# Two units of the first projection moved ahead of the last block of modulation products

## The reference: what is computed

```
shift, scale, gate       = split(silu(c)     @ w_ada + b_ada, 3)      # w_ada: 2048 x 6144
shift_c, scale_c, gate_c = split(silu(c_ctx) @ w_ada + b_ada, 3)
hc = rmsnorm(ctx, g_pre) * (1 + scale_c) + shift_c
zc = hc @ w_in[:, :XBC_W + DT_W]
hx = rmsnorm(x, g_pre) * (1 + scale) + shift
zx = hx @ w_in
```

## Time and profile before

| | |
|---|---|
| three runs | 1981.38 us median (1978.72 to 1981.75) |
| profiled execution | 1981.05 us, its span 1979.2 us |
| PE busy | 1924.8 us, 97% of the span |
| DVE, ACT, POOL busy | 1210.3, 999.0, 102.9 us |
| DMA | 360.39 MB, mean 182 GB/s over the span |
| granted TensorE clock | 0.993 of full speed over the span |
| prefix (until phase B1 starts on PE) | 158.56 us of the span |

### The profile page before, as it was taken

How to read it: one execution, slowest core, us unless ns; L and a number is a source line. 1 busy time by engine, 2 the same in 40 slices (tenths; PEclk the granted TensorE clock), 3 DMA queues, 4 the chain that set the end, 5 groups by cost and what they waited for, 6 DMA issues and landing times.

```text
span 1979.2 us, 27905 instructions
## 1 busy us (share of the span) xinstructions
PE 1924.8 (97%) x10557; PEld 1637.6 (83%) x10557; DVE 1210.3 (61%) x1703; ACT 999.0 (50%) x1464; POOL 102.9 (5%) x117
## 2 busy tenths in 40 slices
PE   5889999989999999999999999999999999999999
PEld 3558888888888888887888998888889999998887
DVE  3335645676548888867866576767555454555554
ACT  5434322344555666754445433566544555556642
POOL 1010000000013344000000000000000000000000
PEclk8999999999999999999999999999999999999999
DMA  9973322347657666657975545545555655555554
GB/s 342 349 243 114 100 75 85 89 146 235 192 168 199 175 179 192 223 181 254 357 252 153 156 139 149 175 135 149 176 188 175 184 164 169 169 162 169 170 190 161
DMA packets 210040, 360.39 MB, mean 182 GB/s; under 512 B 14264, under 2 KB 61776, under 8 KB 209024
## 3 DMA queue, kind: packets, MB, share of 16 engines
q1 hardware_dynamic: 200448, 349.36, 56.7%
q10 hardware_dynamic: 8848, 8.47, 1.8%
q0 software_dynamic: 624, 0.92, 0.2%
HBM read 356.55 MB, written 2.16 MB: 181 GB/s over the span
## 4 chain that ended last, share of the span: by engine, by line
PE 87%; DMA 4%; DVE 3%; SPq 2%; ACT 1%; issue 1%; POOL 1%; ACTq 0%; POOLq 0%; DVEq 0%
PE acc L656 50%; PE acc L643 15%; PE acc L623 10%; DMA raw_first<-in_w_ada 2%; SPq L502 1%; DMA ex_a<-acs_scratch 1%; PE side L1026 1%; DVE w_lo L1912 1%; PE side L901 1%; DVE conv L2079 1%; PE side L718 1%; PE side L796 1%; PE side L893 1%; PE side L954 1%; PE side L623 1%
## 5 line engine op out<-in xcount | busy, mean ns | idle before, releaser
L1912 DVE TENSOR_TENSOR w_lo<-raw,w_hi 128x1024 fp32r<-128x1024 f32 (+1 forms) x552 | 674.5, 1227 | 428.3 <-ACT w_hi L1234 421.7
L1234 ACT CAST w_hi<-raw 128x1024 fp32r<-128x1024 f32 (+1 forms) x544 | 560.8, 1035 | 608.3 <-PE acc L656 414.7
L656 PE MATMUL acc<-w_hi,h_hi 128*128 128x512 f32 (+1 forms) x1312 | 522.6, 398 | 3.2 <-DVE h_lo L2278 1.8
L656 PE MATMUL acc<-w_hi,h_lo 128*128 128x512 f32 (+1 forms) x1312 | 509.1, 388 | 0.0
L656 PE MATMUL acc<-w_lo,h_hi 128*128 128x512 f32 (+1 forms) x1312 | 507.5, 387 | 0.0
L656 PEld LDWEIGHTS acc<-w_hi,h_lo 128*128 128x128 f32 x1312 | 246.3, 188 | 52.4
L656 PEld LDWEIGHTS acc<-w_hi,h_hi 128*128 128x128 f32 x1312 | 246.8, 188 | 50.4 <-DVE h_lo L2278 2.1
L656 PEld LDWEIGHTS acc<-w_lo,h_hi 128*128 128x128 f32 x1312 | 247.0, 188 | 47.0
L643 PE MATMUL acc<-h_hi,w_hi 128*128 128x256 f32 x896 | 258.3, 288 | 7.0 <-DVE w_lo L1912 5.5
L643 PE MATMUL acc<-h_lo,w_hi 128*128 128x256 f32 x896 | 254.4, 284 | 0.0
L643 PE MATMUL acc<-h_hi,w_lo 128*128 128x256 f32 x896 | 254.4, 284 | 0.0
(11 more groups left out here) (409 smaller groups left out, 2031.9 us busy)
## 6 DMA issues: line engine op xcount, KB each, us to landing
raw<-in_w_in SPq DMA_DIRECT2D x184, 512.0 KB, 4.3
raw<-in_w_in_odd SPq DMA_DIRECT2D x128, 512.0 KB, 3.7
raw<-in_w_in_even SPq DMA_DIRECT2D x96, 512.0 KB, 3.7
raw<-in_w_out SPq DMA_DIRECT2D x64, 512.0 KB, 5.0
raw_first<-in_w_ada SPq DMA_DIRECT2D x58, 512.0 KB, 8.8
gate_w<-in_w_ada SPq DMA_DIRECT2D x32, 512.0 KB, 6.7
raw<-in_w_out_even SPq DMA_DIRECT2D x32, 512.0 KB, 3.6
raw<-in_w_out_odd SPq DMA_DIRECT2D x32, 512.0 KB, 3.7
```

What stands on the lines that cost most here:

```text
L656: o = nc.tensor.matmul(ACC[b][:, 0:n], l, r, start=first and kk == 0 and m == 0, stop=last and kk == 1 and m == 2)
L1234: act.copy(WHI[:, u % 4, :, 0:n], RAW[:, u % 4, :, 0:n]).then_inc(hi_ready, 1)
L1912: dve.tensor_tensor(WLO[:, u % 4, :, 0:n], RAW[:, u % 4, :, 0:n], WHI[:, u % 4, :, 0:n].bitcast(F32), ALU.subtract).then_inc(lo_ready, 1)
```

## The change

PE multiplies units 11 and 12 ahead of the products of block 7, and the transposes of block 7 come right behind its products. DVE writes the low part of unit 12 ahead of its copy of block 7's result. In the list of loads units 11 and 12 move ahead of block 6 and unit 13 moves behind block 7, directly ahead of unit 14. POOL starts the loads of the masks and the small vectors at `ada_used` of 32, not 28.

```diff
-for _e in range(3, UPC):
+for _e in range(3, UPC - 1):
     PREFIX += [("ada", _e, v) for v in range(AW4)] + [("w", 0, 2 * _e - 3), ("cols", _e, 0), ("w", 0, 2 * _e - 2)]
+PREFIX += [("w", 0, 11), ("w", 0, 12)] + [("ada", UPC - 1, v) for v in range(AW4)] + [("cols", UPC - 1, 0)]
 PREFIX += [("w", 0, m) for m in range(13, 16)]
 LOADS = [x for x in PREFIX if x[0] == "ada"]
 for _m in range(16):
     _at = len([x for x in PREFIX[:PREFIX.index(("w", 0, _m))] if x[0] in ("ada", "w")])
-    LOADS.insert(_at - (4 if _m < 14 else 0), ("w", 0, _m))
+    LOADS.insert(_at - (4 if _m < 13 else 0), ("w", 0, _m))
...
                 first_lo(2 * e - 3)
-                ada_out(e)
+                if e < UPC - 1:
+                    ada_out(e)
                 halve(2 * e - 2)
                 halve(2 * e - 1)
                 first_lo(2 * e - 2)
+                if e == UPC - 1:
+                    ada_out(e)
                 mod(e)
...
-            pool.wait_ge(ada_used, 28)
+            pool.wait_ge(ada_used, 32)
             pool.dma_start(CON[:, P:], dram["const_a"][:, P:]).then_inc(bc_in, 16)
             ... (three more)
-            pool.wait_ge(ada_used, 32)
             pool.memset(ZB[:], 0.0)
```

## The result

The changed kernel takes 1989.99 us (median of 5 runs, 1989.14 to 1991.64), the kernel before 1981.38 (also 5 runs). The ratio is 1.0049, 95% interval 1.0038 to 1.006; the two medians alone differ by 8.61 us, 0.43%. I had forecast 1985.3 and a range up to 1987.7: the direction is right, the size is more than twice what I gave, and the time lies outside the range.

The account below looks back on a forecast made before the run. PE bounds the span, DMA the prefix from 95 to 105 us. B1 at 162.04 + 0.4 against 158.56 gave +3.9 us, from waits at block 6 and behind block 7: 1985.3 us, range 1980.3 to 1987.7.

Parts of the forecast that it names:

- Masks and clearing: POOL's later loads and clearing: masks hidden with over 8 us of room, clearing costs nothing with some 3 us.
- 8.47 + 0.4: Block 7's products to unit 14: 8.47 us as at block 0, 4.2 of it new waiting, plus 0.4 for the clock.
- The hole: Load queue before block 6: SP held at unit 12, engines dry from about 102.8 us, 3.2 us lost.
- Half the clock on block 6: PE's waits at block 6 halve its clock: fourth quarter 1.87 us to next start, unit 9 loses 0.43 us.
- Block 7 and the masks: Block 7's weights land about 131.5 us, 9 us early; its wait and the masks' cost vanish, products take 3.78 us.
- Tail's clock: Units 13 and 14 after block 7: loss from a lowered clock, lower bound 0, taken as 0.4 us.
- The third rival: Clock stays low in the tail until well into unit 14: +6.1 us, 1987.5 us; chance 0.18.
- The first rival: Queue doesn't run dry, SP not held at unit 12, block 6 late by 2.4 us: -1.0 us, 1980.4; chance 0.12.
- the second: Rival: block 6 isn't late at all, its last quarter landing before 114 us: -3.4 us, 1978.0; chance 0.05.

Follow-up runs that it names:

- a1: Changed kernel with POOL's two clearings made to wait until mod(7) is over: 1987.16 us, ratio 1.0034 to the kernel before.
- a2: Changed kernel with the two copies in mod replaced by additions of two operands, clearing left in place: 1985.13 us, ratio 1.003 to the kernel before.
- a7: Changed kernel with POOL's part undone (masks and vectors at ada_used of 28, clearing at 32): 1986.66 us, ratio 1.0028 to the kernel before.
- a3: Changed kernel with the loads of units 11 and 12 put back behind block 6: 1980.92 us, ratio 1.0001 to the kernel before.
- a4: Changed kernel with loads of units 11 and 12 back behind block 6 and clearing behind mod(7): 1977.53 us, ratio 0.9984 to the kernel before.
- b1: Kernel before with POOL's part alone (masks and vectors loaded at ada_used of 32, clearing behind them): 1973.94 us, ratio 0.9969 to the kernel before.
- a6: Changed kernel with unit 12's load back behind block 6, unit 11's ahead of it, clearing behind mod(7): 1978.23 us, ratio 0.9992 to the kernel before.
- b2: Kernel before with POOL's clearing made to wait for block 7's transposes, so beside mod(7): 1982.96 us, ratio 1.0012 to the kernel before.

## Why the prediction was wrong

B1 was forecast at 162.44 us and came at 167.49. The 5.05 us between them, by the prediction's steps:

- **Masks and clearing: the step that failed.** It said that the clearing costs nothing, with 3 us of room. That was worked out for the one that waits for the clearing (ACT, whose first write into the cleared buffers is at 160.03), and is right; it was not worked out for what runs beside it. The copies in `mod(7)` were held until the clearing ended: 12.34 us from products to unit 14 against 8.47 + 0.4 forecast, 3.47 us more. (The hold itself is 3.7 us, 12.34 against 8.6 in a1 and a2; the 0.4 put down for the clock wasn't needed.) a2, in which nothing is held, took 1985.13 us, close to the forecast, but by luck in part: its B1 was still 2.3 us later than forecast, and the rest of its span 2.4 us shorter than in the kernel before. In the kernel before the clearing was over at 139.48, ahead of the transposes. Two edits brought it beside the copies: transposes right behind the products (a7: 1.8 us held) and four issues ahead of the clearing (a3, changed: 4.2 us). With the hold gone, by either way, the tail was 8.5 to 8.7 us long (a1, a2, a4), as read off block 0. The Trainium skill, "SBUF — State Buffer", section "Who interferes with whom", says that a DVE copy can take a port pair that GpSimd needs too, that whoever is first keeps it for its whole instruction, and that an operation with two SBUF inputs meets only a GpSimd instruction that reads SBUF. The traces agree: 4.18 us for the copy, 0.16 for the addition in its place. They don't show which of the two was first (see what stays open). The prediction had asked only who waits for the clearing.
- **The hole: right, 1.2 us too small.** SP stood still from 96.5 to 103.5 us, as said. From 100 to 108 us the engines moved 2 x (147 + 0 + 141 + 349) = 1274 KB where 2800 were due: 4.4 us lost, not 3.2. I had the queue run at full rate until 102.8 us and "as before" from unit 12's landing on; it was down to 147 GB/s from 100 to 102 us and still at 141 from 104 to 106. Unit 12 landed 4.2 us after its issue, not 3.8, and the last quarter came at 120.66, not 119.43.
- **Half the clock on block 6: right** (on two quarters, of which only the last is on the path), and 0.4 us longer in unit 9 than taken (127.59 - 122.52 = 5.07 against 4.66).
- **Block 7 and the masks.** Landed in time and hidden, as said. But I had put no price on what POOL's loads cost block 7 in the kernel before; b1 shows that POOL's part alone brings B1 5.56 us forward, more than a4 with the new order beside it (3.69).
- **Tail's clock.** 0.4 us was taken; unit 13 took 5.2 us in a4 and 6.6 in a6 where 3.65 is its full speed, which costs nothing up to 1.5 us and, in a6, 1.4 beyond. In the changed kernel unit 14 waited for DVE and not for unit 13, and units 14 and 15 took 9.18 us where 9.08 is full speed. The third rival was real in kind, and in no trace took more than 0.1 us of units 14 and 15.

Together these are 3.5 for the hold, 1.2 for the hole, 0.4 for unit 9 and 0.1 for units 14 and 15, less 0.1 for block 7's products (3.64 us where 3.78 was taken).

The first rival falls by SP's queue, still for 7.0 us, and the second by the last quarter of block 6, at 120.66 us and not before 114. Of the three rivals two were about the order of arrival and one about the clock; none was about two engines at work at once, and so the range ended below the measured time.

What stays open: the copy's record starts 0.46 us ahead of the first clearing's in the changed kernel (147.97 and 148.43), and it was held all the same. In a1 and a4 the copy ran free beside the same last load issue, and there a semaphore kept the clearing from being started. So the hold seems to begin before the clearing's record does; the traces don't show when. I didn't try clearings with a gap between them.

## What to carry to other kernels

When work of an idle engine is moved, look not only at who waits for it, but at what it now runs beside: here 3.8 us of clearing, in nobody's way for its consumer, stopped a copy of two elements on the path. In a queue that goes in order, moving an entry forward moves its wait forward too, and everything behind it waits along; compare the semaphore's time with the time at which the entry would now be reached. And take a change of several parts apart before keeping or dropping it: one of this one's parts gains 0.31% alone.

## What the runs showed that I had not expected

- Small loads spread over the partitions are dear in a full stream: without its 0.08 MB of vectors block 7 comes 2.8 us earlier, without its 0.66 MB of masks 3.0. Each alone costs only 1.1 and 1.3 us; the rest comes with the two together.
- A queue of loads that runs dry loses more than its rest: about 2 us of stillness cost 4.4 us of transfer.
- Two back-to-back clearings (1.88 to 1.89 us each) didn't let the waiting copy in between them, in the three traces where it met the first (changed, a3, b2).
